# A hybrid decoder step on one core: keys transposed on another engine, state work of the linear recurrence a unit later, tiles written out

## The chip, the cores and the metric

One Trainium2 chip, one core. The metric is the time of one execution of the kernel on the device, in microseconds; the time before is the median of three runs. The engines are PE (TensorE), ACT (ScalarE), DVE (VectorE), POOL (GpSimd) and SP (SyncE, which here issues every DMA).

## What is computed

One layer on 2048 prompt tokens and 8 x 4 sample tokens, width 1024, float32. Two branches: an HGRN2 gated linear recurrence with 4 heads of 128 x 128 state, and causal means over windows of 2, 4, 8 and 16 tokens. Cut to what matters:

```python
z = rmsnorm(x) @ w_in                      # q, f, i, g_a, u, g_b, m_a, m_b
fgate = lb + (1 - lb) * sigmoid(f);  k = 1 - fgate;  b = cumsum(log(fgate)) per chunk
S_t = diag(f_t) S_{t-1} + k_t outer v_t ;  o_t = S_t^T q_t      # per head, chunked
o = rmsnorm(o) * silu(g_a)
pooled = window means of u - u;  yb = (pooled @ w_pool) * scale * silu(g_b)
merged = sigmoid(m_a) * (o @ w_proj_a) + sigmoid(m_b) * (yb @ w_proj_b)
y = rmsnorm(x + merged @ w_out)
```

It returns y, the new matrix states of prompt and sample, and the last 15 rows of u.

## The kernel before

**Layout.** Everything is kept transposed: features on the 128 partitions, tokens along the free axis. The 2080 tokens make 5 tiles of T = 416. Tile 0 and the last tile are written out; tiles 1 to 3 are a loop of each engine (`Fori(1, TILES - 1)`). The last tile holds 384 prompt tokens and the 32 sample tokens.

**Units.** A tile is 56 units (`UNITS`), each one 128 x 1024 block of weights: s = 0 to 15 are f, q, i, g of heads 0 to 3, so head h has units 4h to 4h+3; then u and b of the four pooling groups, then m_a, m_b, y, and last out. PE makes a unit as 8 x 3 matmuls of 128x128 by 128x416 (`three`, L487 to L489: high and low parts of weights and data) into one of four PSUM banks Z. The weights of unit n come by DMA (L402, SP) into one of two buffers, ACT makes the high part (`whi`, L761), DVE the low part (`wlo`, L980).

**Steps.** Each engine runs its own list of steps s = 0 to 55, with what belongs to a head placed by formulas such as `s == 4 * h + 7`. ACT's and DVE's step s begins with the split of the weights of unit s + 3, and ACT's split waits until PE has ended unit s - 1. PE's step s begins with `small(t, last, s)`, the small products of that step, and goes on with the unit. SP's step s does its special DMAs first, then waits for `wlo` of unit s and issues the weights of unit s + 2. An engine works in order: what waits holds up all that stands behind it.

**One head on PE** (B4 to B7 are the other four PSUM banks): at s = 4h+7 four transposes of the decayed keys into B7 (L579, L580; three 128x128 blocks `kj4` and the 32 tokens of `e4`), then the scores of chunks into B4 (L519, L523, L524). At 4h+8 the products of keys and values `ktm`, `vtm` into B6 (L542, L544). At 4h+9 `outputs` (L616): scores times values (L623, L626), then, after a wait for the third state update of the head, `s_all` times the decayed queries (L633, L637), into B5. At 4h+12 the sum of squares for the head's norm (L613, L614).

**One head on DVE**: in step 4h+3 the values are transposed in 32 x 32 blocks (L989 to L991). In step 4h+4: the gate (L1012), for h > 0 `updates(h - 1)` (L1106; four calls of `update`, L1098, each decay times state plus product, in a chain; in the last tile three calls behind `sums`, and half of the sample's updates, L1124), `sums` (scan L1020 behind ACT's logf L795, differences L1030), `queries` (L1033: products L1037, L1039, four small copies of factors L1043, a scan L1045, the decayed queries L1050). From step 12 on the normed outputs follow in the same step (L1258, L1260). In step 4h+5 `decayed_keys` (L1073, L1080). In step 4h+7 `scores` (L1065 to L1070; in the last tile also the low part and spread of the sample's values, L1103, L1241). In step 4h+10 the split of the squares (L1317, L1319), in step 4h+13 the low part of the branch output (L1252). The last head's updates are in step 20. ACT copies the transposed keys out of B7 in step 4h+7 (L835, L839) and squares and copies the outputs in step 4h+9 (L848, L849). POOL multiplies the two key tensors (L1476, L1478) in step 4h+4, behind ACT's exponentials.

**Values through memory**: SP at s = 4h+7 stores the block-wise transposed values in four DMAs to `v_blocks` (L458, rows of 128 bytes), and at s = 4h+9 loads them back as `vtm` (L469, L470).

**The end**: the norm over 1024 features of the last tile: last residual (L1170), its square (ACT L933), the sum on PE (L608), ln and exp on ACT (L925, L927) behind a table load, then five blocks scaled on DVE (L1325) and three, already multiplied by their gain (L1290), on POOL (L1497), stored in five DMAs (L447).

Of the kernel before, what the change touches and what calls it, by code (L numbers as in the profile page):

```python
# [33 lines left out]
H = 4  # L34
# [47 lines left out]
for _s in range(NU):  # L82
    for _h in range(H):
        if _s == 4 * _h + 12:
            B4_USES.append(("ssq", _h))
        if _s == 4 * _h + 7:
            B4_USES.append(("scores", _h))
        if _s == 4 * _h + 9:
            B5_USES.append(("o", _h))
# [20 lines left out]
POOL_OUT = 3  # L110
# [4 lines left out]
def step_kernel(nc, xT, w_all, consts, w_pool, s_in, buf_in, yT, sp_out, pp_out, ss_out, ps_out):  # L115
    with ExitStack() as ctx:
# [57 lines left out]
        og = [buf["og0"], buf["og1"]]  # L174
        vt, logf, bc, dd, dl = buf["vt"], buf["logf"], buf["b"], buf["d"], buf["dl"]
# [61 lines left out]
        ats = pad("ats", [SAMPLE])  # L237
        carry = put("carry", [H, P])
# [28 lines left out]

        v_mem = nc.dram_tensor("v_blocks", (T, P), F32, kind="Internal").ap()
# [30 lines left out]
        x0_summed, gained, scaled = sem("x0_summed"), sem("gained"), sem("scaled")  # L299
        kj_made, dq_made, ktm_made = sem("kj_made"), sem("dq_made"), sem("ktm_made")  # L300
# [6 lines left out]
        smasks, so_done, so_made, split_k, split_v = (sem("smasks"), sem("so_done"), sem("so_made"), sem("split_k"),  # L307
                                                      sem("split_v"))
        y_made_pool = sem("y_made_pool")
# [4 lines left out]
        def first(t):  # L314
            return isinstance(t, int) and t == 0
# [49 lines left out]

        def win_value(t, last, g, level, sample=False):
# [10 lines left out]
        def _(sp):  # L377
# [13 lines left out]
            def tile(t, last):  # L391
                for s in range(NU):
                    for h in range(H):
                        if s == 4 * h + 7:
                            values_out(t, h)
                        if s == 4 * h + 9:
                            values_in(t, last, h)
                    n = s + RAW
# [20 lines left out]
                    if last and s in (13, 17, 21, 25):  # L419
                        h = (s - 13) // 4  # L420
# [13 lines left out]
                if last:  # L434
# [6 lines left out]
                    parts = [(POOL_OUT, POOL_OUT + 2), (0, 2), (POOL_OUT + 2, KD - 1), (KD - 1, KD), (2, POOL_OUT)]  # L441
                    for lo, hi in parts:
                        if hi <= POOL_OUT:
                            sp.wait_ge(y_made_pool, hi)
                        else:
                            sp.wait_ge(y_made, t * KD + hi - POOL_OUT)
# [5 lines left out]
            def values_out(t, h):  # L452
# [24 lines left out]
            with sp.Fori(1, TILES - 1) as t:  # L477
# [5 lines left out]
        def _(pe):  # L483
# [7 lines left out]
            def small(t, last, s):  # L491
                for h in range(H):
# [5 lines left out]
                    if s == base + 7:  # L498


                        pe.wait_ge(kj_made, nth(t, KJ * H, KJ * h + KJ - 1))
                        if not h:
                            pe.wait_ge(ybm_made, t * G)
                        elif last:
# [1098 lines left out]
```

## Time and profile before

| | |
|---|---|
| median of 3 runs | 1393.5 us (1393.43 to 1393.59) |
| the profiled execution | 1394.38 us, span 1392.7 us |
| granted clock of PE over the span | 0.997 |
| busy, of the span | PE 1373.0 us, DVE 924.3, ACT 687.4, POOL 246.0 |
| DMA | 187.72 MB, q1 busy 44.1% of 16 engines |

The span is the profiled execution from its first to its last instruction; the run's own time is 1.7 us longer. Busy time counts the time in which at least one instruction of an engine was in work. A timeline row gives the start in us from the beginning of the span, the length, the engine and line, and the idle time before it with what ended it. A row with x3 covers three instructions and lasts from the start of the first to the end of the last. Matmuls overlap: one of 0.35 us begins every 0.19 us.

### The profile page before, as it was taken

To read this page: it belongs to the slowest core of one execution; us is meant where nothing else is said; L and a number is where in the kernel's file an instruction comes from. 1 tells how busy PE (TensorE), PEld (TensorE's weight loads), DVE (VectorE), ACT (ScalarE), POOL (GpSimd) and SP (SyncE) were. 2 spreads that over 40 slices of the span, in tenths; PEclk is the share of its full clock that TensorE was granted. 3 is DMA by queue.
4 is the path that set the end of the run, shared out by engine and by line. 5 is a ranking of instruction groups with operands and counts; after the bars stand their busy time and mean duration, and the time that the engine had idled before them with its cause. 6 is when DMAs were issued, how large, how long until landed. Compare 5 with 4: busy or idle time off the path is not lost.

```text
span 1392.7 us, 22554 instructions
## 1 busy us (share of the span) xinstructions
PE 1373.0 (99%) x8364; PEld 1357.2 (97%) x8364; DVE 924.3 (66%) x1537; ACT 687.4 (49%) x1013; POOL 246.0 (18%) x243
## 2 busy tenths in 40 slices
PE   9999999999999999999999999999999999999996
PEld 7999999999999999999999999999999999999996
DVE  7989655668875456688744557887445688974444
ACT  6565534365663343556643445565434455653332
POOL 2113121110131211111212111112220210130003
PEclk9999999999999999999999999999999999999998
DMA  5433533346335333454263334443533474535337
GB/s 196 129 110 112 204 122 120 94 127 187 103 107 208 121 118 108 130 164 125 92 219 113 114 108 138 154 126 112 198 121 103 124 181 157 162 106 170 121 105 81
DMA packets 97461, 187.72 MB, mean 135 GB/s; under 512 B 49088, under 2 KB 57664, under 8 KB 95680
## 3 DMA queue, kind: packets, MB, share of 16 engines
q1 hardware_dynamic: 97344, 186.16, 44.1%
q8 instruction: 73, 1.20, 0.3%
q14 instruction: 44, 0.36, 0.1%
HBM read 170.72 MB, written 15.42 MB: 134 GB/s over the span
## 4 chain that ended last, share of the span: by engine, by line
PE 90%; DVE 5%; ACT 2%; issue 1%; DMA 0%; DVEq 0%; SPq 0%; ACTq 0%
PE Z L487 28%; PE Z L489 27%; PE Z L488 27%; PE B L633 1%; DVE wlo L980 1%; ACT whi L761 1%; PE B L623 1%; PE B L542 1%; DVE xres L1325 1%; PE B L519 1%; DVE h_b L1020 0%; PE B L579 0%; DVE fac L1043 0%; DMA wraw<-w_all 0%; ACT L855 0%
## 5 line engine op out<-in xcount | busy, mean ns | idle before, releaser
L980 DVE TENSOR_TENSOR wlo<-wraw,whi 128x1024 fp32r<-128x1024 f32 x280 | 367.2, 1312 | 327.3 <-ACT whi L761 327.1
L487 PE MATMUL Z<-hhi,whi 128*128 128x416 f32 x1576 | 554.5, 352 | 1.9 <-DVE wlo L980 1.2
L489 PE MATMUL Z<-hhi,wlo 128*128 128x416 f32 x1576 | 549.3, 349 | 0.0
L488 PE MATMUL Z<-hlo,whi 128*128 128x416 f32 x1576 | 549.3, 349 | 0.0
L761 ACT ACTIVATE whi<-wraw 128x1024 fp32r<-128x1024 f32 x280 | 295.3, 1056 | 428.9 <-PE Z L489 395.7
L487 PEld LDWEIGHTS Z<-hhi,whi 128*128 128x128 f32 x1576 | 295.9, 188 | 4.2 <-issue 3.4
L488 PEld LDWEIGHTS Z<-hlo,whi 128*128 128x128 f32 x1576 | 296.0, 188 | 0.4
L489 PEld LDWEIGHTS Z<-hhi,wlo 128*128 128x128 f32 x1576 | 295.8, 188 | 0.2
L489 PE MATMUL Z<-mhi,wlo 128*128 128x416 f32 x320 | 112.3, 351 | 0.0
L488 PE MATMUL Z<-mlo,whi 128*128 128x416 f32 x320 | 111.9, 350 | 0.0
L487 PE MATMUL Z<-mhi,whi 128*128 128x416 f32 x320 | 111.5, 348 | 0.0
L487 PE MATMUL Z<-yhi,whi 128*128 128x416 f32 x320 | 111.4, 348 | 0.0
L488 PE MATMUL Z<-ylo,whi 128*128 128x416 f32 x320 | 111.4, 348 | 0.0
L489 PE MATMUL Z<-yhi,wlo 128*128 128x416 f32 x320 | 111.4, 348 | 0.0
L1487 POOL TENSOR_TENSOR mA<-mA,mB 128x416 f32<-128x416 f32 x40 | 43.5, 1088 | 343.1 <-DVE mB L1159 343.1
L1476 POOL TENSOR_TENSOR h_e<-h_kin,h_e 128x416 f32<-128x416 f32 x20 | 25.9, 1297 | 366.3 <-ACT h_e L801 366.3
L1432 POOL TENSOR_TENSOR yacc<-yacc,ysq 128x416 f32<-128x416 f32 x34 | 37.0, 1088 | 166.7 <-ACT ysq L933 166.7
L1159 DVE TENSOR_TENSOR mB<-Z,gB 128x416 f32<-128x416 f32 x40 | 23.7, 592 | 57.2 <-PE Z L489 56.9
L1426 POOL TENSOR_TENSOR xacc<-xacc,xsq 128x416 f32<-128x416 f32 x28 | 41.3, 1473 | 114.6 <-ACT xsq L769 114.6
L488 PEld LDWEIGHTS Z<-mlo,whi 128*128 128x128 f32 x320 | 60.1, 188 | 0.6
L487 PEld LDWEIGHTS Z<-mhi,whi 128*128 128x128 f32 x320 | 60.1, 188 | 0.1
L489 PEld LDWEIGHTS Z<-mhi,wlo 128*128 128x128 f32 x320 | 60.1, 188 | 0.0
(234 smaller groups left out, 1672.5 us busy)
## 6 DMA issues: line engine op xcount, KB each, us to landing
wraw<-w_all SPq DMA_DIRECT2D x280, 512.0 KB, 3.5
xres<-xT SPq DMA_DIRECT2D x5, 1664.0 KB, 7.1
xin<-xT SPq DMA_DIRECT2D x4, 1664.0 KB, 7.3
yT<-xres SPq DMA_DIRECT2D x4, 1664.0 KB, 8.1
v_blocks<-h_vt SPq DMA_DIRECT2D x80, 52.0 KB, 2.6
vtm<-v_blocks SPq DMA_DIRECT2D x20, 192.0 KB, 3.7
s<-s_in SPq DMA_DIRECT2D x4, 512.0 KB, 5.8
ss_out<-snew SPq DMA_DIRECT2D x4, 512.0 KB, 5.3
```

Source lines behind the costliest of these rows:

```text
L487: pe.matmul(out, wh, xh, start=first, stop=False)
L488: pe.matmul(out, wh, xl, start=False, stop=False)
L489: return pe.matmul(out, wl, xh, start=False, stop=final)
L519: pe.matmul(B4[rows(g, j), at + CHUNK:(g + 1) * P], e4[:, at:at + CHUNK], after[j], start=True, stop=True)
L542: mm = pe.matmul(B6[:, g * P:(g + 1) * P], ktm[:, g, :], vtm[:, g, :], start=True, stop=True)
L761: act.activation(whi[n % RING][:], raw(t, n)[:], ACT.Copy).then_inc(whi_made, 1)
L980: dve.tensor_tensor(wlo[n % RING][:], raw(t, n)[:], whi[n % RING][:].bitcast(F32), ALU.subtract).then_inc(wlo_made, 1)
L1159: dve.tensor_tensor(out[j % 2][:], z_bank(acc, j)[:, 0:T], gate[j % 3][:], ALU.mult).then_inc(z_sem(acc, j), 1)
L1426: pool.tensor_tensor(xacc[:], xacc[:], xsq[k % 2][:], ALU.add).then_inc(xacc_made, 1)
L1432: pool.tensor_tensor(yacc[:], yacc[:], ysq[j % 2][:], ALU.add).then_inc(yacc_made, 1)
L1476: pool.tensor_tensor(e2[:], kin[h % 2][:], e2[:], ALU.mult).then_inc(k_made, 1)
L1487: pool.tensor_tensor(mA[j % 2][:], mA[j % 2][:], mB[j % 2][:], ALU.add).then_inc(merged, 1)
```

## The change

- **Keys.** `decayed_keys` goes on with a transpose in 32 x 32 blocks of `kj4` and, but for the last tile, of the 32 tokens of `e4`, into a new tile `kt` (which shares its bytes with `logf`). SP stores it at s = 4h+9 in four DMAs to `k_blocks` (`keys_out`) and loads it back at s = 4h+11 as `ktm` (`keys_in`), behind PE's products of the head before. PE's transposes and ACT's copies go, but for the one transpose of the sample's 32 tokens in the last tile.
- **State work.** PE: products of keys and values from s = 4h+8 to 4h+9, outputs from 4h+9 to 4h+10. DVE: updates(h) to step 4h+9, for every head, behind the step's weight split and ahead of `decayed_keys(h + 1)`; they read their decays from a copy `dg`, made in `queries`. ACT squares and copies the outputs in step 4h+10; DVE splits the squares in step 4h+11. SP loads the values at s = 4h+10. In the last tile the sample's values are split in step 4h+8, and its updates stand in steps 4h+9 and 4h+10.
- **Banks.** The pooling products take B7, B6 in turn, not B6, B7.
- **Loops.** Tiles 1 to 3 are written out on all engines.
- **The end.** The last residual, its square, the sum, ln and exp are made in two halves of 208 tokens, with the table loaded ahead of the squares; DVE scales all eight blocks, POOL none.

```diff
@@ SP
-                        if s == 4 * h + 9:
+                            keys_out(t, last, h)
+                        if s == 4 * h + 10:
                             values_in(t, last, h)
+                        if s == 4 * h + 11:
+                            keys_in(t, last, h)
...
+            def keys_out(t, last, h):
+                n = t * H + h
+                rows_out = PT if last else T
+                sp.wait_ge(kt_made, n + 1)
+                if n:
+                    sp.wait_ge(ktm_landed, k_value(t, last, h - 1) if h else 32 * n)
+                for a in range(4):
+                    sp.dma_start(k_mem[0:rows_out, a * CHUNK:(a + 1) * CHUNK].rearrange("(c i) j -> i c j", i=CHUNK),
+                                 kt[a * CHUNK:(a + 1) * CHUNK, 0:rows_out].rearrange("p (c j) -> p c j", j=CHUNK)
+                                 ).then_inc(k_kept, 16)
+            def keys_in(t, last, h):
+                n = t * H + h
+                sp.wait_ge(k_kept, n * 64 + 64)
+                sp.wait_ge(p_done, t * H + h * (3 if last else 1))
+                sp.dma_start(ktm[:, 0:NG, :], k_mem[0:PT].rearrange("(g p) v -> p g v", p=P)).then_inc(ktm_landed, 16)
+                if not last:
+                    sp.dma_start(ktm[0:SAMPLE, 3, :], k_mem[PT:T]).then_inc(ktm_landed, 16)
@@ PE
-                        pe.wait_ge(kj_made, nth(t, KJ * H, KJ * h + KJ - 1))
...
-                        transposes(B7, kj4[:].rearrange("p g j n -> p (g j n)"), tk_done, e4)
+                        pe.wait_ge(kj_made, nth(t, KJ * H, KJ * h + 1))
...
-                    if s == base + 8:
-                        pe.wait_ge(ktm_made, nth(t, H, h))
+                    if s == base + 9:
+                        pe.wait_ge(ktm_landed, k_value(t, last, h))
...
-                    if s == base + 9:
+                    if s == base + 10:
                         outputs(t, last, h)
@@ PE, the last tile's norm
+                    for i, (bank, c) in enumerate(zip((B5, B6), TAIL)):
+                        pe.wait_ge(tail_squared, i + 1)
+                        pe.matmul(bank[:, c], ones_r[:].bitcast(F32), ysq[(KD - 1) % 2][:, c], start=False,
+                                  stop=True).then_inc(tail_summed, 1)
@@ ACT
+                act.wait_ge(k_kept, 64 * (t * H + h))
                 act.activation(logf[:], sf[h % 2][:], ACT.Ln, bias=lb0[:, h:h + 1],
...
-                        if s == 4 * h + 9:
+                        if s == 4 * h + 10:
                             act.wait_ge(o_done, nth(t, H, h))
@@ DVE
+                dve.tensor_copy(dg[h % 2][:], dec[:, :, DG]).then_inc(dg_made, 1)
...
+                dve.wait_ge(k_kept, 64 * (t * H + h))
+                dve.wait_ge(kj_made, nth(t, KJ * H, KJ * h + KJ - 1))
+                ins = dve.transpose(kt[:, 0:PT], kj4[:].rearrange("p g j n -> p (g j n)"))
+                if not last:
+                    ins = dve.transpose(kt[:, PT:T], e4[:, PT:T])
+                ins.then_inc(kt_made, 1)
...
-                    if s % 4 == 2 and 10 <= s <= 22:
-                        h = (s - 10) // 4
+                    if s % 4 == 3 and 11 <= s <= 23:
+                        h = (s - 11) // 4
                         dve.wait_ge(osq_made, nth(t, H, h))
...
-                            if h and not last:
-                                updates(t, last, h - 1)
                             sums(t, last, h)
-                            if h and last:
-                                updates(t, last, h - 1)
                             queries(t, h)
+                        if s == 4 * h + 9:
+                            updates(t, last, h)
+                            if last and h == H - 1:
+                                sample_updates(t, h, 0)
                         if s == 4 * h + 5:
-                            decayed_keys(t, h)
+                            decayed_keys(t, last, h)
+                            if last and h:
+                                sample_updates(t, h - 1, 0)
...
-                        if s == 4 * h + 8 and h == H - 1:
-                            updates(t, last, h)
-                        if s == 4 * h + 9 and last:
-                            for b in range(4, NB):
-                                sample_update(t, h, b)
+                        if s == 4 * h + 10 and last:
+                            sample_updates(t, h, 4)
...
+                    for c in TAIL:
+                        dve.tensor_tensor(xres[:, KD - 1, c], z_bank("out", KD - 1)[:, c], xres[:, KD - 1, c],
+                                          ALU.add).then_inc(tail_made, 1)
+                    output(t, range(KD))
@@ every engine
-            with dve.Fori(1, TILES - 1) as t:
+            for t in range(1, TILES - 1):
                 tile(t, False)
```

## Rows read from the trace of the kernel before

**Rows 1.** The page, part 1: busy us, share of the span and instructions.
```profile
PE 1373.0 (99%) x8364; PEld 1357.2 (97%) x8364; DVE 924.3 (66%) x1537; ACT 687.4 (49%) x1013; POOL 246.0 (18%) x243
```

**Rows 2.** Waits of PE: waiter <- releaser: total us, times, longest.
```profile
PE B L633 <- DVE carry L1098: 2.4, 3, 1.5
```

**Rows 3.** Timeline, PE, tile 2, head 1: start us, us, line, operation, tiles, count.
```profile
610.34 0.49 PE L579 MATMUL B<-ident,kj 128*128 128x128 f32 x3
...
610.87 0.27 PE L519 MATMUL B<-qr,h_e 128*32 128x96 f32 x2
```

**Rows 4.** Timeline, PE, tile 2, s = 8 to 10.
```profile
594.21 0.83 PE L542 MATMUL B<-vtm,ktm 128*128 128x128 f32 x6
...
599.59 0.83 PE L623 MATMUL B<-at_sb,vtm 128*128 128x128 f32 x6
...
600.40 0.91 PE L633 MATMUL B<-q,s_all 128*128 128x128 f32 x6
...
601.29 0.43 PE L487 MATMUL Z<-hhi,whi 128*128 128x416 f32 x1
```

**Rows 5.** Timeline, DVE, tile 2, steps 7 to 9; in brackets the idle before.
```profile
590.97 1.22 DVE L980 TENSOR_TENSOR wlo<-wraw,whi 128x1024 fp32r<-128x1024 f32 x1
...
595.50 1.23 DVE L980 TENSOR_TENSOR wlo<-wraw,whi 128x1024 fp32r<-128x1024 f32 x1 [0.84 <-ACT whi L761]
...
598.33 0.34 DVE L1098 SCALAR_TENSOR_TENSOR s_all<-carry,dec,B 128x128 f32<-128x128 f32 x1
...
599.73 1.02 DVE L1020 TENSOR_TENSOR_SCAN h_b<-smask,h_logf 128x416 f32<-128x416 f32 x1
...
605.78 1.22 DVE L980 TENSOR_TENSOR wlo<-wraw,whi 128x1024 fp32r<-128x1024 f32 x1
```

**Rows 6.** Groups by form, DVE: busy us, mean ns of one, idle before.
```profile
L989 DVE STREAM_TRANSPOSE h_vt<-Z 128x256 f32<-128x256 f32 x20 | 8.8, 438 | 0.1
```

**Rows 7.** Timeline, DVE: the four factor copies, tile 2 and last tile.
```profile
602.80 2.11 DVE L1043 COPY fac<-h_e 128x12 f32<-128x12 f32 x4
...
1150.42 0.38 DVE L1043 COPY fac<-h_e 128x12 f32<-128x12 f32 x4
```

**Rows 8.** The page, part 6, DMA issues: KB each, median us to landing.
```profile
v_blocks<-h_vt SPq DMA_DIRECT2D x80, 52.0 KB, 2.6
vtm<-v_blocks SPq DMA_DIRECT2D x20, 192.0 KB, 3.7
```

**Rows 9.** Timeline, PE, ACT and DVE, tile 2, steps 12 and 13.
```profile
616.16 0.35 PE L613 MATMUL B<-sqh,ones_r 128*128 128x416 f32 x1
...
619.14 0.74 ACT L795 ACTIVATE h_logf<-h_sf,lb 128x416 f32<-128x416 f32 x1
...
620.56 1.02 DVE L1020 TENSOR_TENSOR_SCAN h_b<-smask,h_logf 128x416 f32<-128x416 f32 x1
...
627.74 1.22 DVE L980 TENSOR_TENSOR wlo<-wraw,whi 128x1024 fp32r<-128x1024 f32 x1
628.88 0.58 DVE L1252 TENSOR_TENSOR ylo<-h_og,yhi 128x416 fp32r<-128x416 f32 x1
```

**Rows 10.** Timeline, PE and DVE, tile 0, head 1; DVE, last tile.
```profile
70.98 0.35 PE L613 MATMUL B<-sqh,ones_r 128*128 128x416 f32 x1
...
82.99 1.21 DVE L980 TENSOR_TENSOR wlo<-wraw,whi 128x1024 fp32r<-128x1024 f32 x1
...
1162.23 1.29 DVE L1241 TENSOR_TENSOR vms<-vs,bmask 96x512 fp32r<-96x512 f32 x2
```

**Rows 11.** Timeline, PE, first matmul of tiles 2 and 3.
```profile
556.54 0.45 PE L487 MATMUL Z<-hhi,whi 128*128 128x416 f32 x1 [0.69 <-issue]
...
829.81 0.45 PE L487 MATMUL Z<-hhi,whi 128*128 128x416 f32 x1 [1.20 <-DVE wlo L980]
```

**Rows 12.** Timeline, DVE, the end of the kernel.
```profile
1380.17 0.59 DVE L1170 TENSOR_TENSOR xres<-Z,xres 128x416 f32<-128x416 f32 x1 [1.13 <-PE Z L489]
...
1383.88 5.31 DVE L1325 SCALAR_TENSOR_TENSOR xres<-xres,cst,yrs 128x416 f32<-128x416 f32 x5 [3.12 <-ACT yrs L927]
```

More of the change, by code:

```diff
@@ L174, in step_kernel @@
         og = [buf["og0"], buf["og1"]]
+        kt = put("kt", [T], F32, hg[names.index("logf")])
         vt, logf, bc, dd, dl = buf["vt"], buf["logf"], buf["b"], buf["d"], buf["dl"]
@@ L237, in step_kernel @@
         ats = pad("ats", [SAMPLE])
+        dg = [pad(f"dg{i}", [NG]) for i in range(2)]
         carry = put("carry", [H, P])
@@ L314, in first @@
         def first(t):
-            return isinstance(t, int) and t == 0
+            return t == 0
         def rows(g, j):
@@ L364, in p_value, with k_value @@
             return t * H + h * (3 if last else 1) + i + 1
+        def k_value(t, last, h):
+            return 32 * t * H + (16 if last else 32) * (h + 1)
         def win_value(t, last, g, level, sample=False):
@@ L418, in tile @@
                         sp.dma_start(exts[:, :, :, 0:BUF], buf_in).then_inc(buf_landed, 16)
-                    if last and s in (13, 17, 21, 25):
-                        h = (s - 13) // 4
+                    if last and s in (14, 18, 22, 26):
+                        h = (s - 14) // 4
                         sp.wait_ge(s_made, s_value(t, last, h, NG + NB - 1))
@@ L575, in small @@
                     y_squares(t - 1, False)
-            def transposes(bank, src, done, rest):
-                for g in range(NG):
-                    pe.transpose(bank[:, g * P:(g + 1) * P], src[:, g * P:(g + 1) * P], ident[:])
-                pe.transpose(bank[0:SAMPLE, 3 * P:4 * P], rest[:, PT:T], ident[:]).then_inc(done, 1)
             def sample_products(h, bank, v):
@@ L750, in _ @@
             tile(0, False)
-            with pe.Fori(1, TILES - 1) as t:
+            for t in range(1, TILES - 1):
                 tile(t, False)
@@ L969, in _ @@
             tile(0, False)
-            with act.Fori(1, TILES - 1) as t:
+            for t in range(1, TILES - 1):
                 tile(t, False)
@@ L1109, in updates, with sample_updates @@
                     update(t, last, h, g)
-                if last:
-                    for b in range(4):
-                        sample_update(t, h, b)
+            def sample_updates(t, h, at):
+                for b in range(at, at + 4):
+                    sample_update(t, h, b)
             def sample_update(t, h, b):
@@ L1302, in tile @@
                     y_split(t, True)
-                    residual(t, KD - 1)
-                    output(t, range(POOL_OUT, KD))
+                    dve.wait_ge(acc_done, acc_ready(t, "out", KD - 1))
+                    for c in TAIL:
+                        dve.tensor_tensor(xres[:, KD - 1, c], z_bank("out", KD - 1)[:, c], xres[:, KD - 1, c],
+                                          ALU.add).then_inc(tail_made, 1)
+                    output(t, range(KD))
             def y_split(t, last):
@@ L1406, in _ @@
             tile(0, False)
-            with dve.Fori(1, TILES - 1) as t:
+            for t in range(1, TILES - 1):
                 tile(t, False)
@@ L1491, in tile @@
                         y_sum(t, j)
-                if last:
-                    pool.wait_ge(gained, POOL_OUT)
-                    pool.wait_ge(yrs_made, t + 1)
-                    for j in range(POOL_OUT):
-                        pool.tensor_tensor(xres[:, j, :], xres[:, j, :], yrs[:], ALU.mult).then_inc(y_made_pool, 1)
             for value, m in ((1.0, ones[:]), (0.0, ident[:]), (1.0, cmask[:]), (1.0, cmask_s[:]), (1.0, bmask[:]),
@@ L1546, in _ @@
             tile(0, False)
-            with pool.Fori(1, TILES - 1) as t:
+            for t in range(1, TILES - 1):
                 tile(t, False)
```

101 lines of the change are left out of this document (53 added, 48 removed).

## The prediction

> **What bounds the kernel now.** The page's table of busy time comes first: PE is busy for 1373.0 of 1392.7 us [rows 1]. The reader is to see that only two things can change the time: work taken off PE's stream, and gaps put into it. The table of who waited for whom, for PE alone, comes second: its largest entry inside the tiles is 2.4 us in three waits of the output products (L633) for the state updates (L1098), all in the last tile [rows 2]. The waits name the hand-over on which the kernel is already nearly late, and the change touches exactly that one. The timeline of tile 2 comes third, to measure how far ahead of PE its servants run.
>
> **The clock of the argument.** PE walks through units s = 0 to 55; before each it runs the small products of that s. Two units with a break before the first take 610.34 - 601.29 = 9.05 us, so 4.52 us each [rows 3, 4]. Products of keys and values plus the unit behind them take 599.59 - 594.21 = 5.38 us, and the first half of the output products, which needs no state, 600.40 - 599.59 = 0.81 us [rows 4]. ACT's and DVE's step s begins when PE has ended unit s-1, since ACT's high part of the weights waits for that; DVE's split of step 8 started at 595.50, 0.84 us after DVE was free [rows 5], and PE's s = 8 at 594.21 [rows 4]. So DVE's step 4h+8 is tied to PE's s = 4h+8 in the new kernel too.
>
> **Transposes off PE.** Three transposes of the keys and one of the short block run from 610.34 to 610.87, 0.53 us [rows 3]. In tiles 0 to 3 all four go, for four heads: 16 x 0.53 = 8.5 us; in the last tile three of four go, 4 x 0.40 = 1.6 us, an estimate by their share. PE is busy throughout, so all of it is on the path: -10.1 us. The copies of the result on ACT go as well; ACT is half idle, so that is worth nothing.
>
> **Transposes on DVE.** A transpose of 128x256 takes 438 ns [rows 6]; 128x384 and the short block are put at 1.5 times that, 0.66 us. The bounds are 0.44 us and, if each of the two took a full 0.44 and the wait for the decayed keys showed, 1.1 us; I take 0.66 since the shape only grows by half. The new copy of the decays is like one of four small copies that take 0.38 us together when nothing disturbs them, so 0.1 us [rows 7]. Together 0.76 us a head, against 0.84 us that DVE was waiting ahead of step 8 [rows 5]. They are hidden as long as that cover holds; on its own this would cost nothing.
>
> **The keys through memory.** Four stores in the shape of the values' (2.6 us from issue to landing) and a load in the shape of theirs (3.7 us) [rows 8], queued on SP. SP issues the load only behind the weight load that follows DVE's split of step 4h+7. In tile 2 that split ends near 590.97 + 1.14 = 592.1 [rows 5, 9]; with 0.76 us more of work ahead of it 592.9, an estimated 1.2 us for SP to issue what stands before and the load itself, and 3.7 us to land: 597.8. PE wants it at the new s = 9, 594.21 - 0.53 + 4.52 = 598.2. So it is on time by 0.4 us in head 0. Waiting behind SP's new waits are weight loads, which are wanted two units later, and the values' load, which has more room than the keys'. I cost it at nothing, from 0 to some 2 us a head (the queue could be that much slower with twice the small pieces in it); what would be late is then the product of keys and values, and a part of this hides behind the next wait.
>
> **The updates a unit later: the step that decides.** Before, updates(h) ran on DVE in step 4h+8, ahead of the scan and the factors of the next head, and PE needed them at s = 4h+9. Now PE needs them at s = 4h+10, and DVE makes them in step 4h+9, behind all of step 4h+8. But step 4h+8 is the longest of all: in tile 2 DVE's step 8 runs from 595.50 to 605.78, 10.3 us, more than two units of PE [rows 5].
>
> Head 0 in tile 2. PE's need, no products at s = 8 now: 594.21 + 4.52 + 5.38 + 0.81 = 604.92. DVE: step 9 began at 605.78; without the updates 1.40 us earlier (598.33 to 599.73 [rows 5]), with the copy of the decays 0.1 later; then the weight split 1.14 us (627.74 to 628.88 [rows 9]) and three of four updates, 1.1 us: 606.7. PE is late by 1.8 us, and by 2.3 us since it comes 0.53 us earlier without the transposes while DVE, with its 0.84 us of cover used up, doesn't.
>
> Head 1. PE starts s = 12 at 616.16, and the sum of squares there adds 0.38 us (two matmuls of a Z matmul's length, 9.05/48 us each): need 616.16 + 0.38 + 10.71 = 627.25. DVE: here taking out the updates doesn't pay in full, because the scan then waits for ACT's logf, which ends at 619.88, and the scan stood at 620.56: 0.68 us earlier, not 1.4. Step 13 so begins at 627.74 - 0.68 + 0.1, and split 1.14, the low part of y 0.5 [rows 9] and three updates 1.1 follow: 629.9. Wait: 2.65 us. The anchor moves with PE, so this isn't softened by PE being earlier or later. Head 2 has the same steps: 2.65 us. Head 3 has no scan and no factors in step 20 and waits for nothing.
>
> A loop tile: 2.3 + 2.65 + 2.65 = 7.6 us of new waits, less the 2.1 us of transposes: +5.5, three times: +16.5 us. Tile 0, by head 1: need 70.98 + 11.09 = 82.07; DVE 82.99 - 0.68 + 0.1 + 1.14 + 0.5 + 1.1 = 85.15; wait 3.1 us (the scaling adds to the step) [rows 10], three times, less 2.1: +7.2 us. Last tile: the spread of the sample's values, 1.29 us [rows 10], moves from step 4h+7 into the long step 4h+8, of which 0.6 hides the wait for logf: 2.65 + 0.7 = 3.35, three times 10.0, less the 2.4 that these waits cost already [rows 2] and 1.6 of transposes: +6.0 us. Bounds of one wait: 1.0 us (the copies below undisturbed) and 4 us (transposes and split both disturbed by POOL). Sum of the tiles: +29.7 us.
>
> **Squares a unit later.** They move from the step before the scores' step into it, still one step ahead of PE's use, behind a split that may wait for its weights; PE gets 0.8 us of slack less. Nothing, as PE waits longer at s = 4h+10.
>
> **Tiles written out.** PE idled 0.69 us and 1.20 us at the two jumps back of its loop [rows 11]; with the 0.16 us by which a matmul's 0.35 us overlaps its successor each, 2.2 us. Without a jump the gap is that between units elsewhere, none: -2.2 us. The other engines have the same jumps off the path.
>
> **Tail.** From the last residual to the first scaled block 1380.17 to 1383.88, 3.7 us in a chain at full width [rows 12]; two halves overlapped on DVE, ACT and PE, with the table loaded ahead: I take -0.7 us (0 to -1.5). Then five blocks on DVE took 5.31 us beside POOL's three, 1.06 each; eight alone at the residual's 0.59 [rows 12] are 4.7 us: -0.6, and one store fewer after the last, -0.3. Tail -1.6 us (from +3, if eight cost 1.06 each, to -2.8).
>
> **Sum.** +29.7 - 2.2 - 1.6 = +26 us. The profiled execution took 1394.4 us around its span of 1392.7; the median of the runs is 0.9 us below. 1393.5 + 26 = 1419.5, rounded to 1420 us.
>
> **A rule on the copies.** Four small copies of the factors take 2.11 us in the loop tiles and 0.38 us in the last, where the updates stand ahead of them [rows 7]. So DVE is held up there by something that is over by then, and POOL's two key products run at that place. The Trainium skill, SBUF - State Buffer, section "Who interferes with whom", says that Vector and GpSimd share one port pair as an exclusive lock, and that the second to come is blocked outright. The trace agrees, by the 2.11 against 0.38. By that rule, if the two came apart in the new order, the copies would be short.
>
> **The rivals.**
> *Copies undisturbed.* If the new order let POOL finish first, each long step would be 1.73 us shorter: 15 x 1.73 = 26 us less, 1394 us, no change. Against it: scan, exponentials and POOL's products keep their distances when the updates are gone. For it: the last tile of before. 7%.
> *Updates in time (the other side).* If DVE entered step 4h+9 by 2.65 us earlier than I work out, say because the long step shrinks or PE's s = 4h+10 comes later, the waits vanish, the 2.4 us in the last tile too: -10.1 - 2.4 - 2.2 - 1.6 = -16.3, 1377 us. For it: DVE has 4.5 us more until the use than it had. Against it: step 9 began at 605.78, already past the 604.92 at which PE will want the result. It decides at a step 4h+8 of some 7.6 us. 12%.
> *Keys late.* If the load lands 2 us after PE wants it, heads 0 to 2 lose nothing (the products' delay fits into the wait that follows), head 3 loses 2 us in five tiles, and first heads that come on top a little: +10, 1430 us. The Trainium skill, DMA: Bandwidth & Descriptors, section "Why small descriptors are slow (HBM only)", speaks for it: pieces of this size pay a fixed overhead each; no row here shows what twice as many cost. 15%.
> *The edit doesn't do what it says.* PE's transposes leave the code and the order of waits is plain; under 1%, put with the others.
>
> **How the numbers follow.** Forecast 66%, keys late 15%, updates in time 12%, copies undisturbed 7%. The range 1396 to 1434 takes in the forecast with waits of 1.2 to 3.5 us and the late keys, and leaves out the case at 1377, that at 1394 and a little above. About 0.2% (2.8 us) is what a measurement can tell from no change. Faster 0.14, same 0.03, slower 0.83.
>
> **What the new profile would show.** PE waits at the line of L633 for the updates, some 15 times, 2 to 3.5 us each, in heads 0 to 2 and not in 3; no transposes of keys in tiles 0 to 3; DVE's updates behind a weight split; no gap at tile starts; eight blocks at 0.6 us at the end. I am wrong if the updates of head 1 end within 11 us of PE's sum of squares at s = 12, or if PE waits at L542 for the keys' load.

## The result

| | before | changed |
|---|---|---|
| median | 1393.6 us (1393.4 to 1394.0) | 1457.3 us (1451.7 to 1460.4) |
| ratio, 95% interval | | 1.0447 (1.0433 to 1.0461) |
| span of the profiled execution | 1392.7 us | 1458.7 us |
| granted clock of PE over the span | 0.997 | 0.979 |

The span and the clock are those of one profiled execution, 1460.4 us, the longest of the five. Of the kernel with filler (below) one execution of four took 1725.6 us at a granted clock of 0.752, and its figures are those of the other three.

The kernel is 63.7 us slower. The forecast was 1420 us (1396 to 1434): the right direction, by the mechanism named, and less than half of its size. What is new in the two rows of the table that the forecast didn't speak of: the changed kernel's own times lie 8.7 us apart where those of before beside them lie within 0.5 (2 to 3 us beside the later runs), and its clock is lower.

The page of the changed kernel, part 1, answers to [rows 1]:

```profile
PE 1393.5 (96%) x8292; PEld 1370.8 (94%) x8292; DVE 940.8 (64%) x1594; ACT 679.9 (47%) x980; POOL 242.1 (17%) x240
```

Two things are to be seen. PE's idle time (span less busy) grew from 19.7 to 65.2 us. And its busy time grew by 20.5 us although 72 matmuls fewer run (8292 against 8364): the same work took longer.

The waits of PE, answering to [rows 2] (waiter, what it waited for, total us, times, longest):

```profile
PE B L664 <- DVE s_all L1143: 31.5, 12, 3.8
PE B L664 <- DVE carry L1143: 9.7, 3, 3.7
PE B L518 <- issue: 4.9, 5, 1.8
PE B L571 <- DMA ktm<-k_blocks: 4.7, 6, 1.6
PE B L780 <- DVE ones_r L1378: 2.7, 1, 2.7
```

The first two rows are the output products (L633 before, L664 now) waiting for the state updates (L1098, now L1143): 15 times, 41.2 us, where there were 3 of 2.4 us. The third is the pooling's product of group 3, once a tile, the fourth the keys' load, both new. The fifth is at the start of the kernel and not new. All idle stretches of PE in the timeline together: 33 of 56.5 us, against 9 of 9.2.

The timeline of DVE in tile 2, head 1, answers to [rows 9]: the step that the forecast worked out (start us, length, line, operation, tiles, count, idle before).

```profile
654.57 1.02 DVE L1057 TENSOR_TENSOR_SCAN h_b<-smask,h_logf 128x416 f32<-128x416 f32 x1 [0.67 <-ACT h_logf L827]
...
657.64 2.12 DVE L1080 COPY fac<-h_e 128x12 f32<-128x12 f32 x4
...
660.07 0.17 DVE L1086 COPY dg<-dec 128x3 f32<-128x3 f32 x1
...
661.75 1.22 DVE L1017 TENSOR_TENSOR wlo<-wraw,whi 128x1024 fp32r<-128x1024 f32 x1
662.88 0.58 DVE L1298 TENSOR_TENSOR ylo<-h_og,yhi 128x416 fp32r<-128x416 f32 x1
663.39 0.34 DVE L1143 SCALAR_TENSOR_TENSOR s_all<-carry,dg,B 128x128 f32<-128x128 f32 x1
663.76 0.73 DVE L1143 SCALAR_TENSOR_TENSOR s_all<-s_all,dg,B 128x128 f32<-128x128 f32 x2
...
666.15 0.58 DVE L1128 STREAM_TRANSPOSE kt<-kj 128x384 f32<-128x384 f32 x1
666.65 0.17 DVE L1130 STREAM_TRANSPOSE kt<-h_e 128x32 f32<-128x32 f32 x1
```

And PE beside it:

```profile
650.82 0.35 PE L644 MATMUL B<-sqh,ones_r 128*128 128x416 f32 x1
...
664.55 0.94 PE L664 MATMUL B<-q,s_all 128*128 128x128 f32 x6 [2.50 <-DVE s_all L1143]
```

DVE enters step 13 at 661.75, 10.93 us after PE's sum of squares at s = 12 (the forecast: 627.16 - 616.16 = 11.0). Behind it stand the weight split, the low part of y and three updates, and PE waits 2.50 us for the last of these. The scan waits 0.67 us for logf, as worked out.

The place that the forecast didn't look at is what PE does after such a wait. PE, tile 1, head 0:

```profile
352.94 1.65 PE L664 MATMUL B<-q,s_all 128*128 128x128 f32 x6 [2.35 <-DVE s_all L1143]
354.38 0.47 PE L668 MATMUL B<-h_q,s_all 128*128 128x32 f32 x2
354.67 0.69 PE L518 MATMUL Z<-hhi,whi 128*128 128x416 f32 x1
355.16 0.55 PE L519 MATMUL Z<-hlo,whi 128*128 128x416 f32 x1
355.51 0.55 PE L520 MATMUL Z<-hhi,wlo 128*128 128x416 f32 x1
355.85 0.55 PE L518 MATMUL Z<-hhi,whi 128*128 128x416 f32 x1
```

The six products take 1.65 us instead of 0.94 (row above, 664.55), and the matmuls of the unit start every 0.35 us instead of every 0.19. The stretch by windows (us, busy and count of PE, PEld, DVE, ACT, POOL, then the granted clock, DMA share, GB/s):

```profile
330.00:345.00 15.00, 14.28 (x118) 13.62 (x118) 13.50 (x28) 6.18 (x8) 0.00 (x0) 1.00 0.65 170
350.00:360.00 10.00, 7.65 (x31) 7.32 (x31) 6.98 (x17) 2.78 (x5) 0.00 (x0) 0.66 0.48 129
400.00:410.00 10.00, 7.51 (x49) 7.39 (x48) 9.69 (x23) 5.94 (x11) 3.66 (x3) 1.00 0.15 54
```

The clock there is 0.66 of full speed, that is the lower of its two levels (1.2 GHz) for about two thirds of the 10 us and 2.4 GHz for the rest. The third row holds a wait of 2.49 us too (at 408.04) and has 1.00: not every wait is followed by a fall. Taken over windows of 5 us up to PE's last products, the changed kernel loses 27.2 us of clock (one less the granted clock, times 5 us, summed), in 20 windows, all at or just behind waits for the updates; weighed by PE's busy time in each window instead of its 5 us, it is 23.5 us. Before loses none. Of the 15 waits for the updates 11 have such a window behind them. The four without are 2.49 to 2.51 us long, and two with one are 1.68 and 1.95 us: the length alone doesn't tell.

### The profile page after: what moved, and what is told of

It is laid out like the page before. It is cut to its first block, busy times and chain, and to the rows that moved or that the text cites. A ratio compares the mean times of both kernels' runs of the same rounds, so it can differ in the third digit from the quotient of the medians.

```text
span 1458.7 us, 21285 instructions
## 1 busy us (share of the span) xinstructions
PE 1393.5 (96%) x8292; PEld 1370.8 (94%) x8292; DVE 940.8 (64%) x1594; ACT 679.9 (47%) x980; POOL 242.1 (17%) x240
## 3 DMA queue, kind: packets, MB, share of 16 engines
q8 instruction: 66, 1.08, 0.3%
## 4 chain that ended last, share of the span: by engine, by line
PE 75%; DVE 15%; ACT 4%; issue 3%; DMA 2%; SPq 1%; DVEq 0%; ACTq 0%
PE Z L518 23%; PE Z L520 23%; PE Z L519 23%; DVE fac L1080 3%; DMA wraw<-w_all 2%; DVE wlo L1017 2%; ACT L882 1%; DVE h_b L1057 1%; PE B L664 1%; DVE s_all L1143 1%; DVE xres L1369 1%; ACT whi L792 1%; DVE h_d L1067 1%; DVE h_q L1074 1%; SPq L480 1%
## 5 line engine op out<-in xcount | busy, mean ns | idle before, releaser
L518 PE MATMUL Z<-hhi,whi 128*128 128x416 f32 x1576 | 562.4, 357 | 0.0
L519 PE MATMUL Z<-hlo,whi 128*128 128x416 f32 x1576 | 556.4, 353 | 0.0
L520 PE MATMUL Z<-hhi,wlo 128*128 128x416 f32 x1576 | 556.3, 353 | 0.0
L518 PEld LDWEIGHTS Z<-hhi,whi 128*128 128x128 f32 x1576 | 301.7, 191 | 2.2 <-issue 0.8
L519 PEld LDWEIGHTS Z<-hlo,whi 128*128 128x128 f32 x1576 | 302.0, 192 | 1.1
L520 PEld LDWEIGHTS Z<-hhi,wlo 128*128 128x128 f32 x1576 | 301.0, 191 | 1.0
L664 PE MATMUL B<-q,s_all 128*128 128x128 f32 x120 | 22.4, 333 | 41.2 <-DVE s_all L1143 31.5
```

Of the source, the lines that this page charges most:

```text
L518: pe.matmul(out, wh, xh, start=first, stop=False)
L519: pe.matmul(out, wh, xl, start=False, stop=False)
L520: return pe.matmul(out, wl, xh, start=False, stop=final)
L664: pe.matmul(B5[:, g * P:(g + 1) * P], s_all[:, g, :], q4[h % 2][:, g].rearrange("p j n -> p (j n)"), start=False, stop=False, skip_group_c ...
```

## Experiments

### Updates in time, everything else changed

Each head's updates go back to DVE's step 4h+8, between the sums and the queries; the last head's stay where the changed kernel has them.

```diff
                             sums(t, last, h)
+                            if h:
+                                updates(t, last, h - 1)
                             queries(t, h)
...
-                        if s == 4 * h + 9:
+                        if s == 4 * h + 9 and h == H - 1:
                             updates(t, last, h)
```

> The changed kernel with one edit: DVE makes the updates of heads 0 to 2 in step 4h+8, between the sums and the queries of the next head, and no longer in step 4h+9. Theory (the added time is PE's 15 waits for the updates, 41 us, and the lower clock that follows such waits, some 27 us): both go, the granted clock is back at 0.995 or more, PE waits for updates under 3 us, and the time is 1385 to 1391 us, below the kernel before. Rival (the keys' way through memory slows the matmuls and lowers the clock): only the 41 us go, the clock stays near 0.98, 1412 to 1420 us.

Measured: 1405.4 us (1404.6 to 1409.1), ratio 1.0088 (1.0073 to 1.0104), clock 0.998. Its waits of PE:

```profile
PE B L571 <- DMA ktm<-k_blocks: 5.8, 7, 2.5
PE B L644 <- DVE at_sb L1108: 5.8, 6, 1.9
PE B L518 <- issue: 4.9, 5, 1.8
PE B L622 <- DVE snew L1171: 4.4, 3, 1.6
```

The waits for the updates are gone and the clock with them is back (no window under 0.99 up to PE's last products): 52 us of the 64 hang on this one hand-over. But the time is neither theory's: 12 us above the kernel before remain, and PE's idle stretches are 27 of 26.2 us, none with a fall of the clock behind it. L644 is the sum of the squares at s = 4h+12. What it waits for are DVE's scores of the next head (L1108), which free its bank B4 and in the new order stand behind the split of the squares in the same step. L622, with 1.2 us more at L539, is in the last tile, where PE waits for the sample's updates. The later runs are about these 12 us.

### The updates ahead of the weight split

The updates stay in step 4h+9 but stand ahead of the split of its weights, so PE's wait should shrink by the split and the low part of y.

```diff
+                    if s % 4 == 1 and 9 <= s <= 17:
+                        updates(t, last, (s - 9) // 4)
                     if (s + AHEAD < NU or not last) and not (first(t) and s + AHEAD < FIRST):
                         split(t, s + AHEAD)
```

> The changed kernel with the updates of heads 0 to 2 at the head of DVE's step 4h+9, ahead of the weight split and the low part of y, instead of behind them. Theory: each wait shortens by what no longer stands ahead, 1.14 us in head 0 and 1.64 us in heads 1 and 2, from 41 us in all to about 19; if the clock follows the length of the waits, most of its 27 us come back: 1410 to 1420 us. Rival (the clock falls for another reason): 22 us less, 1433 to 1438 us.

Measured: 1417.9 us (1417.5 to 1420.7), ratio 1.0169 (1.0154 to 1.0185), clock 0.994. PE's waits for the updates:

```profile
PE B L664 <- DVE s_all L1143: 13.2, 11, 1.8
PE B L664 <- DVE carry L1143: 5.6, 3, 2.6
```

18.8 us instead of 41.2: 22.4 us less idle, and 39.4 us less time. So a microsecond of these waits costs more than itself. The lost clock is 5.0 us instead of 27.2, in three falls; one of the three (1.7 us) stands behind a wait for the keys (2.57 us at 55.62) and not for the updates. The waits for the updates are now 1.8 us at most outside the last tile.

### Matmuls into the wait

Twelve matmuls whose result nobody reads are put ahead of the wait, in heads 0 to 2 of tiles 0 to 3. They add work and bring the end of no wait nearer; what they can give back is the clock, and at most some 0.25 us a wait that PE needs to start again (worked out below), 3 us in all.

```diff
+                if not last and h < H - 1:
+                    for _ in range(FILL):
+                        pe.matmul(B7[:, 0:T], ones_r[:], hhi[0][:], start=True, stop=True)
                 pe.wait_ge(s_made, s_value(t, last, h, NG - 1))
```

> The changed kernel with 12 idle matmuls of 128x416 (2.2 us) into a bank that nobody reads, on PE ahead of the wait for the updates, heads 0 to 2, tiles 0 to 3. The waits are filled, not shortened. Theory (a wait lowers the clock afterwards): the end of each wait stays where it is, within 0.5 us, the clock stays at 1.0 in tiles 0 to 3, and the 18 to 22 us that it costs there come back: 1434 to 1441 us. Rival (the clock falls because of the keys' traffic or of the order of work, not of idle time): no change, 1455 to 1460 us.

Measured: 1442.5 us (1440.8 to 1445.6), ratio 1.0357 (1.0338 to 1.0376), clock 0.993. Tile 1, head 0 again, PE:

```profile
343.81 2.53 PE L663 MATMUL B<-hhi,ones_r 128*128 128x416 f32 x12
346.17 0.83 PE L668 MATMUL B<-q,s_all 128*128 128x128 f32 x6
```

```profile
350.00:360.00 10.00, 10.00 (x95) 9.67 (x94) 5.51 (x12) 3.90 (x5) 0.00 (x0) 1.00 0.72 182
```

The first products after the filled wait take 0.83 us, as at full clock [rows 4], and the windows behind have 1.00. The clock still falls in the last tile, where nothing was filled in: 6.9 us lost. In 12 places work that is thrown away gave 15 us back between the medians and 13 between the means (expected: 16 to 23, so just under it; the rival's "no change" is refuted). So the clock's loss is a cost of its own beside the wait. Weighed by PE's busy time the lost clock fell from 23.5 to 5.9 us, 17.6 less. That is to be compared with the two profiled executions, whose spans are 19.6 us apart (1458.7 and 1439.1). The filler takes 29.7 us of PE's stream, and PE's idle stretches are 29.2 us less (27.3 instead of 56.5), so filler that outlasts its wait costs 0.5 us in sum; the rest of the matmuls take 20.0 us less, the 17.6 of the clock and some 2.4 that fit the restarts.

### Tiles written out; and the new end with it

Both parts alone on the kernel before. First only the loops:

```diff
-            with pe.Fori(1, TILES - 1) as t:
+            for t in range(1, TILES - 1):
                 tile(t, False)
```

> The kernel before with its tiles 1 to 3 written out and nothing else. Theory: the gaps of 0.69 and 1.20 us at the two jumps back go, with the 0.16 us of overlap each: 2.2 us less, 1391.3 us. Rival (the jumps cost nothing that the longer program doesn't cost elsewhere): 1393.5 us or more.

Measured: 1391.8 us (1391.4 to 1393.1), ratio 0.9986 (0.9977 to 0.9995): -2.0 us, with -2.2 forecast. PE's two idle stretches at the starts of tiles 2 and 3 [rows 11] are gone. The Trainium skill, Runtime: NRT & Kernel Launch, section "Instruction fetch mechanics", says that "Branching breaks sequential prefetch"; the runs agree, by the 2.0 us for two jumps.

Then the end as well (the last residual and the norm in halves, five stores, all eight blocks on DVE):

```diff
-                    residual(t, KD - 1)
-                    output(t, range(POOL_OUT, KD))
+                    for c in TAIL:
+                        dve.tensor_tensor(xres[:, KD - 1, c], z_bank("out", KD - 1)[:, c], xres[:, KD - 1, c],
+                                          ALU.add).then_inc(tail_made, 1)
+                    output(t, range(KD))
```

> The kernel before with its tiles written out and with the new end (last norm in halves, all eight blocks scaled on DVE), nothing else. Theory: 2.0 us from the loops, as the run with the loops alone showed, and the 1.6 us that the prediction gave the end: 1389 to 1391 us. Rival (eight blocks on one engine take longer than five and three on two): 1392 us or more.

Measured: 1389.6 us (1389.4 to 1391.2), ratio 0.9969 (0.9957 to 0.9981), as expected. The end of it, DVE, answers to [rows 12]:

```profile
1377.95 0.66 DVE L1312 TENSOR_TENSOR xres<-Z,xres 128x208 f32<-128x208 f32 x2 [1.13 <-PE Z L486]
1380.79 4.59 DVE L1335 SCALAR_TENSOR_TENSOR xres<-xres,cst,yrs 128x416 f32<-128x416 f32 x8 [2.19 <-ACT yrs L931]
```

From the last residual to the first scaled block 2.84 us instead of 3.71, and eight blocks in 4.59 us where five beside POOL took 5.31. -2.1 us, with -1.6 forecast. This is the fastest version of all: 4 us below the kernel before, and 68 below the changed one.

### The keys' load earlier

On top of the updates in time: SP issues the keys' load one step earlier, right behind the values'.

```diff
                             values_in(t, last, h)
-                        if s == 4 * h + 11:
-                            keys_in(t, last, h)
+                            keys_in(t, last, h)
```

> The first experiment's kernel (updates early) with the keys read back one step of SP earlier, right behind the values. Theory (PE's 7 waits for the keys' load, 5.8 us, come from its place in SP's queue): they go with the restart of PE after each, 6 to 8 us less, 1397 to 1400 us. Rival (the stores before it set its time, and SP now holds back weights): 1404 us or more.

Measured: 1410.9 us (1409.7 to 1413.3), ratio 1.0126 (1.0110 to 1.0141), 5.5 us slower than without the edit. The theory fell, and the time is the rival's. PE waits for no keys any more, but its waits at the sum of the squares rose from 5.8 to 8.9 us and those for the sample's updates from 5.6 to 6.9, and in sum its idle stretches are what they were, 26.2 us in both. The loss is in the clock: 6.8 us of it, where the kernel without the edit lost none. The falls stand behind waits of 2.18 and 2.33 us at the sum of the squares (118.84 and 668.23; without the edit 1.88 and 1.68 us) and of 1.61 and 1.20 us in the last tile, each with another of 0.68 and 1.28 us 2 to 3 us before. ACT waited 90.7 us for weights instead of 62.0 (29.5 before), so the weight loads do come later, as the rival had it; that this is what lengthens PE's waits isn't shown apart. The keys' place in SP's order was no mistake that could be mended by moving it.

### Keys transposed on PE again, with early and with late updates

PE transposes the keys and ACT copies them out, as before; no memory, no transposes on DVE. Once with the updates in time, once with the updates late as in the changed kernel.

```diff
-                        if s == 4 * h + 9:
-                            keys_out(t, last, h)
...
-                        if s == 4 * h + 11:
-                            keys_in(t, last, h)
...
+                        transposes(B7, kj4[:].rearrange("p g j n -> p (g j n)"), tk_done, e4)
...
-                pe.wait_ge(ktm_landed, k_value(t, last, h))
+                pe.wait_ge(ktm_made, nth(t, H, h))
```

> The first experiment's kernel (updates early) with the keys transposed on PE and copied by ACT as in the kernel before, so without the way through memory and without DVE's transposes; the unit-later order, the written-out tiles and the new end stay. Theory: 10.1 us of PE's work come back, the waits for the keys' load (5.8 us) go, and those for the scores on DVE (5.8 us) shrink to 1 or 2: 1400 to 1406 us, so the keys' new way is worth next to nothing here. Rival (the new way pays its 10 us in full): 1413 to 1417 us.

> The changed kernel with the keys transposed on PE and copied by ACT as in the kernel before; the updates stay in step 4h+9. Theory (the waits for the updates and the lower clock behind them have nothing to do with the keys' memory traffic): the 15 waits stay at 38 to 42 us, the clock stays at 0.975 to 0.99, and the time is 1453 to 1463 us. Rival (the traffic lowers the clock): clock 0.995 or more, 1432 to 1440 us.

Measured: in time 1399.1 us (1398.7 to 1400.8), ratio 1.0039 (1.0023 to 1.0054), clock 0.998. Late 1458.2 us (1456.4 to 1460.2), ratio 1.0460 (1.0444 to 1.0476), clock 0.981, with 25.5 us of lost clock and none in the other. PE's waits for the updates in the late one:

```profile
PE B L666 <- DVE s_all L1145: 29.2, 12, 3.7
PE B L666 <- DVE carry L1145: 10.6, 3, 3.6
```

The first is 0.9 us under what was expected, the second inside. The late updates cost 59.1 us with the keys on PE (39.8 us of waits) and 51.9 with the keys through memory, and the fall of the clock needs no key traffic: the rival that blamed the memory way is out. The memory way itself costs 6.4 us where the updates are in time (1405.4 against 1399.1) and makes no difference that can be told where they are late (1457.3 against 1458.2, inside the spread of either). The transposes that leave PE held its stream for 9.9 us, as forecast. With the updates in time PE's idle stretches are 11.2 us more with the memory way (26.2 against 15.0): 5.8 for the keys' load, 4.7 more at the sum of the squares (5.8 against 1.1), 1.9 more for the sample's updates. With late ones they are 7.0 us more (56.5 against 49.5): 4.7 for the keys' load, and in head 0 the waits for the updates are 13.5 us instead of 10.8.

### The squares a unit later, alone

What was left of 1399.1 above 1389.6 is the new order without its late updates. PE's 4.9 us at the pooled products stood in every run with that order. This run takes the best kernel and moves nothing but the split of the squares.

```diff
-                    if s % 4 == 2 and 10 <= s <= 22:
-                        h = (s - 10) // 4
+                    if s % 4 == 3 and 11 <= s <= 23:
+                        h = (s - 11) // 4
```

> The kernel before with its loops written out and the new end (1389.6 us), and with one part of the head's new order: DVE's split of the head's squares one unit later (step 4h+11); outputs and updates stay where they were. In the changed kernel PE waits 4.9 us in five times for the pooled products of group 3, which the kernel before doesn't. Theory: the later split alone causes these (the split of head 3 now stands in step 23, among the pooling's products, and pushes DVE back past the low part of group 3): about 5 us of PE waits at the pooled products, five times, and 1394 to 1397 us. Rival: the split is only a part, and ACT's later squares and copies (its step 4h+10) push the pooling back; then the waits at the pooled products are under 1 us and the time is 1389 to 1391 us, as without this edit. The prediction put the later squares at nothing, as the rival does for this edit alone.

Measured: 1398.4 us (1396.6 to 1400.0), ratio 1.0034 (1.0022 to 1.0046), clock 0.996. PE's waits, without that at the start of the kernel:

```profile
PE B L484 <- issue: 4.8, 5, 1.8
...
PE B L635 <- DVE carry L1110: 2.4, 3, 1.5
PE B L576 <- DVE kj L1092: 1.0, 1, 1.0
PE B L615 <- DVE at_sb L1082: 0.8, 1, 0.8
```

The five waits are back, in the same size, and the edit costs 8.8 us, more than the 4 to 7 that the theory had. Against the version without it PE's idle stretches grew by 5.6 us (12.7 against 7.1), and 3.4 us of clock were lost where it lost none: 1.7 right behind the 1.81-us wait at 150.53 in tile 0, and 1.7 at the last tile's wait of 1.52 us, which stood there before without a fall. What pushes DVE is in the changed kernel's timeline, DVE, tile 1, steps 23 to 26:

```profile
438.69 1.08 DVE L1361 CAST sqh<-h_osq 128x416 fp32r<-128x416 f32 x1
439.80 1.17 DVE L1363 TENSOR_TENSOR sql_head<-h_osq,sqh 128x416 fp32r<-128x416 f32 x1
440.90 1.28 DVE L1318 TENSOR_TENSOR pooled_lo<-pooled,pooled_hi 128x416 fp32r<-128x416 f32 x1
...
451.63 0.58 DVE L1318 TENSOR_TENSOR pooled_lo<-pooled,pooled_hi 128x416 fp32r<-128x416 f32 x1
```

and PE's, tile 1:

```profile
452.32 0.43 PE L518 MATMUL B<-pooled_hi,wph 128*128 128x416 f32 x1 [0.94 <-issue]
```

The two splits take 1.08 and 1.17 us here, against 0.37 and 0.59 at 647.87 and 648.27, where the pooling isn't under way. They stand in step 23, ahead of the pooling's work, and the low part of group 3 at 451.63 ends at 452.21, just ahead of PE's start at 452.32. That the split causes it is shown by the run. Without the edit all 20 of these casts take 0.36 to 0.38 us; with it nine of them, heads 2 and 3 of tiles 0 to 3 and head 3 of the last, take 1.03 to 1.08. That it is by being drawn out beside POOL, which is busy for 2.24 of the 2.40 us from 438.6 in the changed kernel, is read from these lengths.

## Why the prediction was right and wrong

**What each part cost**, as steps from one kernel to the next:

| kernel | us | step |
|---|---|---|
| before | 1393.6 | |
| tiles written out | 1391.8 | -2.0 |
| new end | 1389.6 | -2.1 |
| squares' split a unit later | 1398.4 | +8.8 |
| rest of the new order, updates in time, keys on PE | 1399.1 | +0.7 |
| updates late | 1458.2 | +59.1 |
| keys through memory | 1457.3 | -0.9 |

The kernel before stood at 1393.4 to 1393.9 us beside these runs, and the first step is against the 1393.8 beside its own. The steps of +0.7 and -0.9 are inside the spreads.

**Right.** *What bounds the kernel*: PE, and the hand-over of the updates as the one that decides. *The waits for the updates*: forecast 42.1 us (three loop tiles of 7.6, tile 0 of 9.3, the last of 10.0), measured 41.2 (21.0, 10.5 and 9.7), in heads 0 to 2 and none in head 3. *Tiles written out*: -2.2 forecast, -2.0 measured. *The end*: -1.6 forecast, -2.1 measured, inside its bounds. *Transposes on DVE*: 0.58 and 0.17 us, forecast 0.66 together; the copy of the decays 0.17 instead of 0.1. *Updates in time* was refuted as a rival, *copies undisturbed* as well: the four copies take 2.12 us in the new order too.

**Wrong, first: the price of a wait.** The sum set a microsecond of waiting at a microsecond of time. The step that failed is the one from the waits to the sum of the tiles: 42.1 us of waits less the 2.4 there already are +39.7 in it, and the runs put +59.1 there, for 39.8 us of waits. Two terms were missing. The larger is PE's clock: from [rows 3, 4] I took the lengths of products at full clock and used them behind waits of 2 to 3.7 us as well. Weighed by PE's busy time, 23.5 us of clock were lost. The smaller is the restart. After a wait the first matmul takes 0.43 us instead of 0.35, the next starts 0.28 us later instead of 0.19, and the 0.16 us by which a predecessor overlapped are lost: 0.25 us a wait, 6.0 us for 24 more of them. I had used the 0.16 us for the loop's jumps and forgotten it for the waits that I added. Together, from the two profiled executions: idle stretches +47.3 us, restarts +6.0, clock +23.5, transposes -10.1, end -2.1, which makes 64.6 of the 66.0 us between the spans. The split between clock and restart is worked out and not measured apart.

That the clock is a cause and not a companion is shown by the filled waits: same hand-over, more work, 13 to 15 us less. That in the changed kernel it is the waits for the updates that bring it down is shown by the runs that shorten them: 41.2, 18.8 and 0 us of these waits go with 27.2, 5.0 and 0 us of lost clock. It is nothing peculiar to these waits: in other runs falls stand behind waits for the keys, at the sum of the squares and at the pooled products too.

**Wrong, second: the squares a unit later**, set at nothing, cost 8.8 us. The argument looked at PE's use at s = 4h+12 and found it covered. It did not ask what stands behind the split on DVE: for head 3 that is the pooling. The cost of a moved step lay with the work that it was moved in front of.

**Wrong, third: the keys through memory**, set at nothing in a range of 0 to 2 us a head, so that the 10.1 us of transposes would be gained in full. The runs give 0.9 us for both together. In head 0 they were late in each tile, by 0.38 to 1.57 us; with a second in the last tile (0.86), 4.7 us in six waits. Here is the one of tile 0:

```profile
53.72 0.94 PE L571 MATMUL B<-vtm,ktm 128*128 128x128 f32 x6 [1.57 <-DMA ktm<-k_blocks]
```

The forecast had them on time by 0.4 us in this head of tile 2, where the wait is 0.50 us; PE's wait for the keys' load is one of the two signs that it named for being wrong. The term that was too small is the load. The forecast took the 3.7 us of the values' load [rows 8], a median, and by the median the keys' load is no slower:

```profile
ktm<-k_blocks SPq DMA_DIRECT2D x20, 192.0 KB, 3.5
k_blocks<-kt SPq DMA_DIRECT2D x64, 52.0 KB, 1.9
```

But in head 0 of tile 2 its second part was issued at 625.12, 0.9 us after the end of DVE's split (1.2 were estimated), and landed at 630.20, 5.1 us later; PE went on at 630.24. In head 0 of tiles 0, 1 and 3 this took 4.4, 5.1 and 5.0 us, in the 12 other heads of tiles 0 to 3 it took 3.4 in the median, and in the last tile the loads took 5.0 to 7.9. The DMA engines were busy for 0.99 of the 5 us from 339, behind the load of tile 1, and for 0.88 of those from 625, against 0.67 and 0.68 in head 1 (from 364 and 648); but the last of these loads took 4.7 us too, so the share alone doesn't tell. The *keys late* rival so had it right that the load is slow, but not where: it priced the wait in head 3, which has none in any tile, and put the first heads at "a little". Its reason, the small pieces, isn't shown: the stores landed in 1.9 us. That a wait at s = 4h+9 fits into the one behind it isn't shown either. In head 0 the waits for the updates are longer with the memory way than without it, by 2.7 us in five tiles, with the waits for the keys in front of them.

**The size of the miss.** The forecast was +26 us and the change +63.7. The waits (+59.1 instead of +39.7) are 19.4 us of the difference, the keys with the transposes (-0.9 instead of -10.1) 9.2, the squares 8.8, and the rest of the new order, the loops and the end 0.4.

**Left open.** Why some waits of 2.5 us are followed by the lower clock (380.56) and others of the same length are not (408.04); and whose traffic slows the keys' load in head 0 and in the last tile.

## What to carry to other kernels

On a kernel whose PE is busy all the time, a new wait costs more than its own length: 40 us of waits here cost 59. Work out both its length and what follows it, and if a step must be late, shorter waits are cheaper by more than their length (22 us less of them gave 39). When a step is moved later, ask of every engine that it touches what is now behind it, not only whether its own result is still in time: a 1-us split moved by one step cost 8.8 us in work that has nothing to do with it. And take a change of many parts apart before judging it: two of its parts alone make a kernel that is 4 us faster than before.

## What the hardware showed that I had not expected

- PE's granted clock fell to its lower level (1.2 GHz of 2.4) for some us after single waits of 1.5 to 3.8 us, in a stream that was otherwise all but always busy. Products of 128x416 then started every 0.35 us instead of every 0.19. The Trainium skill, TensorE: Matmul & The Clock Gate, section "What's actually happening", says that the default state is throttled and activity releases the throttle. The trace agrees in kind: 0.66 in the 10 us from 350 with the wait that ends at 352.94, 1.00 where the same wait is filled with products.
- The same wait need not have the same effect: the 1.80 us at the pooled products of tile 0 are followed by the lower clock with the keys on PE and late updates (163.87; 0.66 in the 5 us from 165) and not in the changed kernel (165.98). The changed kernel's times spread over 8.7 us with clocks of 0.979 to 0.985; that the falls differ between its executions is likely and not shown, since one was profiled.
- Work that nobody reads, put into a wait, made the kernel 13 to 15 us faster.
- A median hides the load that matters: the keys' load, 3.5 us in the median, took up to 5.1 us in the first head of tiles 1 to 3 and up to 7.9 us in the last tile.
- DVE's casts of 128x416 took 1.08 us beside the pooling and 0.37 elsewhere; as with the factor copies [rows 7], 2 to 3 times as long, for operations that are small.
